# A two-layer encoder trunk on one core: another task order, four probability buffers and moved modulation steps

## The reference

```python
mod = c_act @ ada_w[l] + ada_b[l]                    # 6 * D values from D, once a layer
sh1, sc1, g1, sh2, sc2, g2 = jnp.split(mod, 6, axis=-1)
h = rmsnorm(x, g) * (1 + sc1) + sh1
proj = h @ w_in                                      # q, k, v: 16 heads of 64, and the forget gate
s = q k^T / 8 + F[q] - F[k]                          # F: running sum of log_sigmoid; causal
p = softmax(s);  y = (p @ v) @ w_o;  x = x + g1 * y
h = rmsnorm(x, g') * (1 + sc2) + sh2;  x = x + g2 * conv_ffn(h)
```

## Time and profile before

| | |
|---|---|
| median of three runs | 2566.41 us (2560.12 to 2568.66) |
| time of the profiled execution | 2563.79 us |
| its span, first to last instruction | 2562.0 us |
| TensorE, VectorE, ScalarE, GpSimd busy | 93%, 62%, 45%, 44% of the span |
| mean granted TensorE clock | 0.96 of full |

### The profile page before, as it was taken

One profiled execution on the slowest core, in us unless ns is written; L12 is line 12 of the kernel. 1 busy time (PEld: TensorE's weight loads), 2 busy tenths in 40 slices (PEclk: granted clock), 3 DMA queues, 4 the chain that ended last, 5 costly groups with the idle time before them and its releaser, 6 DMA issues.

```text
span 2562.0 us, 31418 instructions
## 1 busy us (share of the span) xinstructions
PE 2371.5 (93%) x11208; PEld 1968.7 (77%) x11208; DVE 1583.9 (62%) x2579; ACT 1150.2 (45%) x1933; POOL 1133.5 (44%) x1568
## 2 busy tenths in 40 slices
PE   5999999898998999999999988987989999999996
PEld 3878788786777878888888877776777888888884
DVE  5575765757428677777775676774285455554446
ACT  4365564646416333333333375663164334333344
POOL 1411312121144666666666443113446666666660
PEclk8999999998899999999999998987999999999998
DMA  6121222223310333433331122114101111112111
GB/s 246 59 91 54 83 83 63 76 65 99 123 46 28 97 116 119 119 119 117 118 121 58 58 99 64 50 42 173 42 28 55 58 50 50 50 50 64 52 58 66
DMA packets 98731, 205.41 MB, mean 80 GB/s; under 512 B 9856, under 2 KB 59648, under 8 KB 98448
## 3 DMA queue, kind: packets, MB, share of 16 engines
q1 hardware_dynamic: 31808, 109.06, 13.5%
q10 hardware_dynamic: 66768, 94.35, 11.7%
HBM read 185.09 MB, written 16.32 MB: 79 GB/s over the span
## 4 chain that ended last, share of the span: by engine, by line
PE 68%; DVE 16%; ACT 7%; DMA 4%; issue 4%; POOL 1%; ACTq 1%; DVEq 0%; SPq 0%; POOLq 0%
PE bank L882 41%; PE bank L614 16%; DVE ada_acc_f L1622 1%; DVE bank L1700 1%; DVE X L1891 1%; PE bank L810 1%; PE bank L749 1%; PE bank L664 1%; DVE PL L1726 1%; PE bank L775 1%; PE bank L785 1%; PE bank L1064 1%; PE bank L811 1%; PE bank L812 1%; DVE ada_acc L1622 1%
## 5 line engine op out<-in xcount | busy, mean ns | idle before, releaser
L882 PE MATMUL bank<-H,w_spl 128*128 128x512 f32 x3744 | 879.4, 393 | 25.3 <-DVE H L1606 14.6
L882 PEld LDWEIGHTS bank<-H,w_spl 128*128 128x128 f32 x3744 | 704.1, 189 | 182.3 <-issue 16.2
L543 POOL TENSOR_TENSOR w_spl<-w_raw,w_spl 128x256 fp32r<-128x256 f32 x688 | 529.3, 796 | 458.5 <-ACT w_spl L1360 457.0
L614 PE MATMUL bank<-H,w_spl 128*128 128x512 f32 x2016 | 506.1, 401 | 25.2 <-DVE H L1606 11.9
L882 PE MATMUL bank<-TB,w_spl 128*128 128x512 f32 x2112 | 494.8, 390 | 0.4 <-ACT sU L1375 0.4
L614 PEld LDWEIGHTS bank<-H,w_spl 128*128 128x128 f32 x2016 | 379.0, 192 | 107.2 <-issue 18.8
L882 PEld LDWEIGHTS bank<-TB,w_spl 128*128 128x128 f32 x2112 | 395.0, 188 | 83.2 <-issue 1.2
L1360 ACT ACTIVATE w_spl<-w_raw 128x512 fp32r<-128x512 f32 x328 | 201.8, 628 | 530.8 <-PE bank L882 369.4
L486 POOL TENSOR_TENSOR pace<-one_s 128x1 f32<-128x1 f32 x50 | 13.3, 267 | 806.7 <-PE bank L775 377.1
L1891 DVE SCALAR_TENSOR_TENSOR X<-bank,mods,X 128x1024 f32<-128x1024 f32 x176 | 225.0, 1278 | 34.4 <-PE bank L882 34.3
L1884 DVE TENSOR_TENSOR bank<-bank,sU 128x512 f32<-128x512 f32 x80 | 55.9, 699 | 269.4 <-PE bank L882 269.3
(11 more groups left out here) (179 smaller groups left out, 3310.4 us busy)
## 6 DMA issues: line engine op xcount, KB each, us to landing
w_raw<-in_w_stream SPq DMA_DIRECT2D x184, 512.0 KB, 3.7
ada_raw_f<-in_ada_w ACTq DMA_DIRECT2D x192, 128.0 KB, 2.3
ada_raw_a<-in_ada_w ACTq DMA_DIRECT2D x32, 512.0 KB, 3.9
ada_raw<-in_ada_w SPq DMA_DIRECT2D x8, 1024.0 KB, 14.4
negF<-scratch_f ACTq DMA_DIRECT2D x16, 512.0 KB, 3.8
ada_raw_f<-in_kv_ada_w ACTq DMA_DIRECT2D x64, 128.0 KB, 2.5
X<-in_x_t SPq DMA_DIRECT2D x4, 1024.0 KB, 10.8
X<-in_x_t ACTq DMA_DIRECT2D x4, 1024.0 KB, 8.0
```

Source lines behind the costliest of these rows:

```text
L543: last = pool.tensor_tensor(block_at(layer, b, 1, q, q + 256), src[:, q:q + 256], block_at(layer, b, 0, q, q + 256).bitcast(F32), ALU.subt ...
L614: last = pe.matmul(dst, stat(k, a), mov(k, b), start=(k == 0 and a + b == 0), stop=(k == KT - 1 and a == 1))
L882: last = pe.matmul(dst, block_at(layer, b, x, k * P, k * P + P), mov(y), start=(start and x + y == 0), stop=(stop and x == 1), skip_group_ ...
```

## The change

1. `TASKS` has another order: each head's short diagonal tasks stand between long ones.
2. The value matmuls follow three tasks behind the score instead of two (`LAG`), and PF, PH and PL have four buffers instead of three (`NP`).
3. The first 32 k-steps of a group's fill are spread two a task over 16 tasks (`FILL_1`) instead of 3, 2, 3, 2 over 13. The maxima wait for the parts of the projections that they read, not for all of them, and `MAX_T` of the second head begins one task earlier with another pattern.
4. In attention only g1 is made: 64 steps of 128 columns, four a head (tasks 1, 4, 7, 10), each with its own load of 64 KB in two buffers. The other 24 columns are made in the out-projection: 96 steps of 256 columns, twelve ahead of each residual, loads of 128 KB in three buffers, and the sums over partitions behind the second k of the next tile.
5. Around it: `row_max` stands ahead of `v_low` between two groups, the last normalisation of a group and its `log_sums` come one v_step later, ScalarE's squares stand between the new loads, and `v_high` waits for the task of its own key block.

```diff
-TASKS = [(0, kb) for kb in range(4)] + [(1, kb) for kb in range(8)]
+TASKS = [(0, 0), (0, 3), (0, 1), (0, 2), (1, 0), (1, 7), (1, 1), (1, 6), (1, 2), (1, 5), (1, 3), (1, 4)]
-LAG = 2
+LAG = 3
+NP = 4
-MAX_T = [[2, 1, 1, 1, 1, 1, 1, 2, 2, 0, 0, 0], [0, 0, 0, 2, 2, 2, 2, 2, 2, 0, 0, 0]]
+MAX_T = [[2, 1, 1, 1, 1, 1, 1, 2, 2, 0, 0, 0], [0, 0, 2, 1, 2, 1, 2, 1, 2, 1, 0, 0]]
-FILL_1 = [3, 2, 3, 2, 3, 2, 3, 2, 3, 2, 3, 2, 2]
+FILL_1 = [2] * 16
+ADA_T = (1, 4, 7, 10)
+ADA_O = 12
...
# TensorE, maximum
+                if h and c in (0, 8):
+                    pe.wait_ge(qk_lo, 8 if h == 1 else 2 * (4 * (h // 2) + (2 if c == 0 else 3)) + e + 1)
                 if c == 0:
                     if h:
-                        pe.wait_ge(qk_lo, 2 * (4 * (h // 2) + 4))
                         pe.wait_ge(m_rows, h)
...
# TensorE, the loop over the tasks
-                    if t == 11:
-                        ada_cols(ada_acc_a, 2, 8 * (4 * g + hl + 1), 1, 0)
+                    if t == 11 and hl % 2:
+                        ada_cols(ada_acc_a, 1, 8 * (2 * g + hl // 2 + 1), 1, 0)
...
+            def ada_of_tile(m):
+                for c in range(12 * m // 8, 12 * (m + 1) // 8):
+                    ada_cols(ada_acc_o[:, c % 2], 2, ADA_STEPS_O + 8 * (c + 1), 2, 2 * c)
...
# TensorE, out_proj, in the loop over k of tile m
+                        if layer == 0 and k == 1 and m:
+                            ada_of_tile(m - 1)
...
+                if layer == 0:
+                    ada_of_tile(7)
...
# ScalarE
+            def load_ada_o(j):
+                if j < 8 * ADA_O:
+                    if j >= 3:
+                        act.wait_ge(ada_step, ADA_STEPS_O + j - 2)
+                    col = M_SH2 * P + 256 * (j // 8)
+                    act.dma_start(ada_raw_o[:, j % 3], ada_w[0, j % 8 * P:j % 8 * P + P, col:col + 256]
+                                  ).then_inc(adao_in[j % 3], 16)
...
-                    act.wait_ge(pv_ps, 4 * NT * g - 7 + j)
+                    act.wait_ge(pv_ps, 4 * NT * g - NT + TASKS.index((1, j)) + 1)
...
+                    if T and (T - 1) % NT in ADA_T:
+                        load_ada(16 * g + 4 * ((T - 1) // NT) + ADA_T.index((T - 1) % NT) + 2)
...
+            act.wait_ge(o_lo, 8)
+            for j in range(3):
+                load_ada_o(j)
+            for m in range(8):
+                if m:
+                    squares(1)(m - 1)
+                for j in range(12 * m, 12 * m + 12):
+                    load_ada_o(j + 3)
...
# VectorE
+            def ada_beside(m):
+                for j in range(12 * m, 12 * m + 12):
+                    chunk = j // 8
+                    dve.wait_ge(adao_in[j % 3], 16 * (j // 3 + 1))
+                    if j % 8 == 0 and chunk >= 2:
+                        dve.wait_ge(ada_ps, ADA_0 + KT + chunk - 1)
+                    ada_steps(ada_acc_o[:, chunk % 2], lambda k: ada_raw_o[:, j % 3], ADA_STEPS_O + 8 * chunk, ks=[j % 8])
...
# VectorE, out_proj
                 for m in range(8):
+                    if layer == 0:
+                        ada_beside(m)
                     dve.wait_ge(wo_ps, 8 * layer + m + 1)
...
             out_proj(0)
+            dve.wait_ge(ada_ps, N_ADA_PS)
+            V_.tensor_tensor(mods[:, M_SH2:M_L1], bank(2, 0, 2 * ADA_O), modb[:, M_SH2:M_L1], ALU.add).then_inc(ada_ev, 1)
```

More of the change, by code:

```diff
@@ L199, in program @@
         negF = at("negF", [P, 2, S], F32, 184)
[L200 to L206, removed]
+        PH = [at(f"PH{i}", [P, HALF], F32R, 192 + 2 * i) for i in range(NP)]
+        PF = [at(f"PF{i}", [P, HALF], F32, 200 + 2 * i) for i in range(NP)]
+        PL = [at(f"PL{i}", [P, HALF], F32R, 200 + 2 * i) for i in range(NP)]
+        O_st = at("O_st", [P, S], F32, 208)
+        rec = at("rec", [P, HALF], F32, 212)
+        ada_raw_a = at("ada_raw_a", [P, 2, P], F32, 214)
+        ada_acc_a = at("ada_acc_a", [P, P], F32, 215)
+        ada_raw_o = at("ada_raw_o", [P, 3, 256], F32, 210)
+        ada_acc_o = at("ada_acc_o", [P, 2, 256], F32, 213)
         O_rawA = at("O_rawA", [P, 4, S], F32, 128)
@@ L312, in program @@
         ada0_in = [sem(f"ada0_in{i}") for i in range(8)]
-        ada_in = sem("ada_in")
+        adaa_in = [sem(f"adaa_in{i}") for i in range(2)]
+        adao_in = [sem(f"adao_in{i}") for i in range(3)]
         ada0_step = sem("ada0_step")
@@ L400, in program @@
         y_out = [sem(f"y_out{i}") for i in range(2)]
-        N_ADA_A = 4 + 4 * NG
-        ADA_STEPS_A = 8 * 4 * NG
+        ADA_0 = 4
+        N_ADA_PS, N_ADA_A = ADA_0 + KT + ADA_O, ADA_0 + KT + 1
+        ADA_STEPS_O = 8 * KT
+        ADA_STEPS_A = ADA_STEPS_O + 8 * ADA_O
         O_OUT_A = 16 * 7
@@ L815, in _ @@
             for c in range(NM):
-                maximum(0, c, 4)
+                maximum(0, c, ADA_0)
                 if c < 4:
@@ L829, in _ @@
                     for c in maxima_at(MAX_V, tt):
-                        maximum(4 * g, c, 4 + 4 * g)
+                        maximum(4 * g, c, ADA_0 + 2 * g)
                     if tt == 6:
@@ L839, in _ @@
                         for c in maxima_at(MAX_T[hl], t):
[L840 removed]
+                            maximum(4 * g + hl + 1, c, ADA_0 + 2 * g + hl // 2)
                     if hl < 3 and t == 10:
                         turn_max(4 * g + hl + 1)
[L843 to L844 removed]
+                    if t == 11 and hl % 2:
+                        ada_cols(ada_acc_a, 1, 8 * (2 * g + hl // 2 + 1), 1, 0)
                     for n, k in qk_steps(g, T):
@@ L1152, in load_negf, with load_ada @@
                               ).then_inc(nf_in[h % 2], 16)
-            def load_ada(piece, half):
-                act.dma_start(ada_raw_a[:], ada_w[0].rearrange("(k p) n -> p k n", p=P)[
-                    :, 4 * half:4 * half + 4, 2048 + 256 * piece:2304 + 256 * piece]).then_inc(ada_in, 16)
+            def load_ada(j):
+                if j < 8 * KT:
+                    if j >= 2:
+                        act.wait_ge(ada_step, j - 1)
+                    col = M_G1 * P + P * (j // 8)
+                    act.dma_start(ada_raw_a[:, j % 2], ada_w[0, j % 8 * P:j % 8 * P + P, col:col + P]
+                                  ).then_inc(adaa_in[j % 2], 16)
+            def load_ada_o(j):
[5 more added lines that the diff above has]
+                                  ).then_inc(adao_in[j % 3], 16)
             def qk_high(n, e):
@@ L1284, in _ @@
                         load_negf(4 * g + hl + 3)
[L1285 to L1290, removed]
+                    if g == 0 and T == 0:
+                        load_ada(0)
+                        load_ada(1)
+                    if T and (T - 1) % NT in ADA_T:
+                        load_ada(16 * g + 4 * ((T - 1) // NT) + ADA_T.index((T - 1) % NT) + 2)
                     if g == NG - 1 and T in (25, 26, 27, 28):
@@ L1474, in ffn @@
                 high(FT // 2 - 1, 1)
-            for k in range(8):
-                squares(1)(k)
+            squares(1)(7)
             root(1)
@@ L1742, in behind, with ada_one, ada_mods @@
                         normalize(chunk)
[L1744 to L1752, removed]
+            def ada_one(j):
+                dve.wait_ge(adaa_in[j % 2], 16 * (j // 2 + 1))
+                ada_steps(ada_acc_a[:], lambda k: ada_raw_a[:, j % 2], j // 8 * 8, ks=[j % 8])
+            def ada_mods(b):
+                dve.wait_ge(ada_ps, ADA_0 + b + 1)
+                V_.tensor_tensor(mods[:, M_G1 + b:M_G1 + b + 1], bank(1, 0, 1), modb[:, M_G1 + b:M_G1 + b + 1],
+                                 ALU.add).then_inc(ada_ev, 1)
+            def ada_beside(m):
[5 more added lines that the diff above has]
+                    ada_steps(ada_acc_o[:, chunk % 2], lambda k: ada_raw_o[:, j % 3], ADA_STEPS_O + 8 * chunk, ks=[j % 8])
             def o_low(k):
@@ L1796, in _ @@
                         low_task(g, T - 1)
-                    if t == 0 and hl:
-                        ada_mods(4 * g + hl - 1)
+                    if t == 0 and hl == 2:
+                        ada_mods(2 * g)
                     if hl < 3:
@@ L1903, in ada_mods @@
                     col = M_KV + 2 * chunk if chunk < 8 else M_L1 + 2 * (chunk - 8)
-                    dve.wait_ge(ada_ps, N_ADA_A + chunk + 1)
+                    dve.wait_ge(ada_ps, N_ADA_PS + chunk + 1)
                     V_.tensor_tensor(mods[:, col:col + 2], bank(4, 0, 2), modb[:, col:col + 2], ALU.add).then_inc(ada_ev, 1)
```

31 lines of the change are left out of this document (15 added, 16 removed).

## The result

The changed kernel takes 2574.45 us (median of 12 runs, 2570.56 to 2577.45), the kernel before 2566.1 us (12 runs): the ratio is 1.0033, 95% interval [1.0024, 1.0042], so it is 0.3% slower. I had forecast 2541.

The account below looks back on a forecast made before the run. TensorE, busy 93% of the span, was taken as the bound, so only its idle or low-clock time could be won. Span 2562.0 - 57 (attention) + 32 (out-projection) = 2537, on the median 2541 us; range 2514 to 2563.

Parts of the forecast that it names:

- the sum for the attention: Attention: gains of all sixteen heads add to 59.2 us, taken as 57 because of the stage's end and ScalarE's waits.
- Three engines level at 20: Attention heads 5, 9, 13: TensorE, ScalarE and VectorE each have about 20 us of work; 22.2 us a head forecast.
- lower bound, 28 us: Attention: the least gain, nothing but VectorE's saved 2.8 us in each of the ten heads that TensorE does not lead.
- the three-buffer round: Out-projection: three steps take 3.0 us, not 1.8, since each load waits for a freed buffer; twelve steps 10.8.
- the place behind X: Out-projection start: modulation loads queue behind four 1 MB X loads, so residual 0 ends at 695.1 us instead of 683.2.
- +32: Out-projection: forecast cost in us, taken between +30 (13.5 us a tile) and +35 (14.2); bounds +22 and +48.
- the weight load's 0.7: Out-projection: one 512 KB weight load a tile delays the modulation loads, adding 0.7 us to the 13.5 us cycle.
- The attention wins little: Rival: ScalarE and VectorE level with TensorE, and LAG 3 only moves the wait; gain 32, cost 32, 2566 us; chance 0.14.
- Hidden steps: Rival: the moved modulation steps are hidden, out-projection within 5 us of before, time 2514 us; chance 0.14.
- the clock: Rival: stalls keep TensorE at half clock in the out-projection, +95 us, time 2604 us; chance 0.08.
- bad bounds (28 and 48): Smallest attention gain, 28 us, with largest out-projection cost, 48 us: 2586 us, which needs both parts at their worst.

Follow-up runs that it names:

- e2: Changed kernel with the value matmuls two tasks behind the score instead of three, four buffers kept: 2561.1 us, attention 510.9.
- e5: Changed kernel with LAG 2, but row sums, normalisation and sending of a head one task later, where LAG 3 puts them: 2579.0 us, attention 526.7.
- e9: Changed kernel with LAG 3 kept, but row sums, normalisation and sending of a head one task earlier, where LAG 2 puts them: 2556.7 us, attention 510.9.
- e3: Changed kernel with the tasks in the old order, short diagonal tasks last in each half: 2576.1 us, attention 523.1.
- e4: Changed kernel with twelve buffers instead of three for the out-projection's modulation loads, still behind the X loads: 2552.9 us, out-projection 99.6.
- e8: Changed kernel with LAG 2 and twelve buffers for the out-projection's modulation loads, the first twelve issued ahead of X: 2536.0 us, out-projection 94.3.

## Why the prediction was wrong

**The step that failed** is the sum for the attention: 57 us forecast, 24.8 measured. By heads, forecast and then measured:

- 5, 9, 13: 22.2 each; 28.7, 29.2, 28.6. This is 19.9 us of the miss. "Three engines level at 20. I take 22.2" added up each engine's work and let two us stand for the order in their queues. The work was right: in head 5 VectorE was busy 19.1 us and ScalarE 19.9. But these heads have work of all kinds in the same tasks, and I had not put the normalisation, one task later by the lag, beside the evacuations, one piece of which the even fill moves to the same task. I had costed the later row sums at nothing. e2, e5 and e9 show that their place alone is worth 11 to 16 us over the attention. It is not all: with early sums (e9) the three heads still take 25.7, 3.5 more than forecast, without a loss of clock.
- 1: 18; 22.3. The same without fill: 4.3 us. With LAG 2 it takes 19.8, with early sums at LAG 3 21.7.
- 3, 7, 11: 54 each; 57.8. 4, 8, 12: 32 each; 29.8. These go together. The three values that the lag carries over the border of two groups are of 384, 512 and 512 columns, where there were two of 256 and 128; I had counted them at the end of the stage only. At the prices of the prediction they are 1.9 us against 0.7, so 1.2 of the 3.8; e2 (55.8) and e3 (55.2) show that lag and order both have a part in it, and the rest was not taken apart. For the pair, 86.0 forecast, 87.6 measured: 4.8 us of the miss.
- 2, 6, 10: 25.3; 24.9. Right, within the spread.
- 0, 14, 15: 27.3, 20.5, 21; 28.7, 23.0, 23.9. Another 6.8, whose cause is open.

Even the part's lower bound, 28 us, was missed: it took for granted that time freed on an engine is time it can use. Of the 32.2 us that the part fell short, the early place of the sums gives back 10.9. The best attention of any run, 510.9, is still 21 us short of the forecast, and why is not shown.

**The out-projection was right** in its mechanism, and e4 and e8 confirm it: the three-buffer round, and the place behind X. That +32 met +32.0 to the tenth is luck, for small misses cancel. The first residual ended 672.06 - 646.65 = 25.4 us in, against 695.1 - 670.9 = 24.2 forecast. The cycle was 13.6 against 14.2 with the weight load's 0.7 and 13.5 without, and yet the 0.7 was real: four loads issued within 1 us behind a weight load landed after 4.1 to 4.5 us instead of 2.2, and VectorE's waits behind the first came to 37.1 us, 4.6 a tile, where 10.8 - 7.2 + 0.7 = 4.3 had been reckoned. What had been put too long is the step: it took 0.53 us on average (51.3 us in 96) and not 0.60, which is 0.8 a tile.

**The rivals.** "The attention wins little" (0.14), with a gain of 32 and a cost of 32, is what happened, and a little more. Half of its reason was right: the lag moved the wait, 40.1 us for PL to 3.2, and 19.3 and 7.9 for the maxima. But no engine was full in head 5: of its 28.7 us VectorE was busy 19.1, ScalarE 19.9 and TensorE 23.0. "Hidden steps" fell. Of the clock: the granted share in the out-projection fell from 1.00 to 0.91. TensorE waited for VectorE five times there, 5.1, 2.2, 3.9, 2.6 and 5.5 us, and with all but the 2.2 one the clock fell to 1.2 GHz, during the wait or just behind it. The first three of the four:

```profile
665.53:671.24 5.71, 5.71 (x15) 4.65 (x16) 2.27 (x5) 0.00 (x0) 0.00 (x0) 0.50 0.56 184
708.78:715.61 6.83, 5.95 (x16) 4.89 (x17) 4.60 (x8) 1.06 (x1) 0.00 (x0) 0.50 0.63 188
739.50:742.92 3.42, 3.42 (x10) 2.64 (x9) 2.40 (x5) 1.06 (x1) 0.00 (x0) 0.50 0.31 94
```

TensorE: Matmul & The Clock Gate in the Trainium skill (HAM oscillation) would have each wait for data followed by a cold loop; four of the five waits here agree, one does not. The rival had the clock fall, and it did; it was wrong in what that costs. Between the low stretches the clock came back to 1.00, and the pace was VectorE's: no residual waited for TensorE, and the cycle of 13.6 us is what loads and steps explain. With twelve buffers one low stretch is left (clock 0.97), with the first loads ahead of X none (1.00). How much of the 19.8 us that e4 won is the clock was not taken apart.

**The range** ended at 2563. Both parts near their bad bounds (28 and 48) gave 2586; I had called both at once not to be expected, but -24.8 and +32.0, the one past its bound and the other as forecast, gave 2574.

## What to carry to other kernels

Ask of a lag or a shifted step not only which wait it removes but what else moves with it, and write down for each engine what its queue holds in that very task: VectorE, busy two thirds of head 5, was the bound in some of its tasks and idle in others. Work moved beside a long matmul stage is free only if its loads keep up: the steps that run while a load is under way must last longer than it takes to land. With three buffers, each loaded again when its step is done, these were two steps, 2 x 0.53 us against 2.2. And count the bulk loads that stand ahead of the first one.

## What the runs showed of the hardware that I had not expected

A modulation step of 128 columns took 361 ns on average against 534 for one of 256, so half the columns cost two thirds of the time. In the out-projection the DMA engines moved 167 GB/s with three buffers and VectorE waited 44.6 us; with twelve they moved 204 and it waited 7.5. The rate alone did not tell that the loads were late and not too many. And a wait of TensorE cost clock as well as time: behind waits of 2.6 to 5.5 us it ran at 1.2 GHz for 3.4 us or more, in the out-projection and in head 5.
